# RWKV branch of a hybrid decoder step: the samples' 64 rows move into the prompt's last tile

## The reference, cut to what matters

```
def step(s, inp):
    r_t, w_t, k_t, v_t, kk_t, a_t = inp
    sa = jnp.einsum('bhij,bhj->bhi', s, -kk_t)
    s = s * w_t[:, :, None, :] + sa[..., None] * (kk_t * a_t)[:, :, None, :] + v_t[..., None] * k_t[:, :, None, :]
    return s, jnp.einsum('bhij,bhj->bhi', s, r_t)
...
s_fin, o = lax.scan(step, s_prev.astype(F32), xs)
```

## Time and profile before

| | |
|---|---|
| median of three runs | 2222.6 us |
| the profiled execution | 2221.23 us, span 2219.4 us |
| RWKV block, layer 1, first solve to end | 300.2 to 552 us |
| TensorE, share of the span | 92% |
| VectorE | 48% |
| ScalarE | 31% |
| GpSimd | 10% |
| mean granted TensorE clock | 0.964 of full |

### The profile page before, as it was taken

The page is one execution under the profiler, slowest core; times in us unless marked ns, Lnnn a source line. Parts: engine busy times, 40 slices in busy tenths (PEclk is TensorE's granted clock), DMA queues, the critical chain, the costliest instruction groups (busy, mean ns, idle before and its releaser), DMA issues. The chain is left out here.

```text
span 2219.4 us, 55745 instructions
## 1 busy us (share of the span) xinstructions
PE 2049.8 (92%) x24578; PEld 1330.7 (60%) x24578; DVE 1076.1 (48%) x2577; ACT 682.0 (31%) x1853; POOL 226.4 (10%) x225
## 2 busy tenths in 40 slices
PE   8999978997999999999989999789979999999997
PEld 4665667775566566754456656577754665667543
DVE  2016047674566457833320160477745664588333
ACT  1122044443455442310012220444434554423100
POOL 0000000001000024301100000000010000243022
PEclk9999989997999989999999999899979999899999
DMA  5102010000000337732111020100000003377221
GB/s 199 48 1 85 0 40 4 4 4 22 2 1 1 86 149 277 266 124 71 63 59 48 1 85 1 40 4 4 4 23 1 1 1 86 152 282 258 87 78 57
DMA packets 49843, 150.85 MB, mean 68 GB/s; under 512 B 15106, under 2 KB 19458, under 8 KB 40132
## 3 DMA queue, kind: packets, MB, share of 16 engines
q1 hardware_dynamic: 37316, 71.79, 9.7%
q0 software_dynamic: 12288, 75.51, 9.2%
HBM read 129.70 MB, written 12.86 MB: 64 GB/s over the span
## 5 line engine op out<-in xcount | busy, mean ns | idle before, releaser
L373 PE MATMUL psum<-work 128*128 128x368 f32 (+1 forms) x1632 | 515.3, 477 | 8.9 <-DMA work<-w_z 6.6
L373 PEld LDWEIGHTS psum<-work 128*128 128x128 f32 (+1 forms) x1632 | 308.1, 189 | 212.7 <-issue 26.7
L2191 PE MATMUL psum<-work,mixed 128*128 128x512 f32 (+1 forms) x576 | 252.9, 600 | 1.6 <-PEq L1863 1.6
L2191 PEld LDWEIGHTS psum<-work,mixed 128*128 128x128 f32 (+1 forms) x576 | 107.8, 188 | 140.3 <-issue 140.3
L2059 DVE STREAM_TRANSPOSE work<-work 128x1024 f32<-128x1024 f32 x128 | 150.5, 1214 | 0.4 <-issue 0.3
L1635 ACT ACTIVATE work<-psum,work 128x128 f32<-128x128 f32 (+8 forms) x130 | 97.9, 753 | 160.5 <-DVE work L1738 160.0
L1519 PE MATMUL psum<-work 96*128 96x512 f32 (+3 forms) x384 | 139.6, 498 | 3.7 <-ACT work L1635 2.1
L1803 POOL DMA_INDIRECT work<-cache_ckv,pages x64 | 60.7, 948 | 623.4 <-PE psum L1469 386.4
L1963 PE MATMUL psum<-work,ckv 128*64 128x256 f32 x1024 | 118.0, 382 | 0.7 <-ACT ckv L2018 0.7
L1519 PEld LDWEIGHTS psum<-work 96*128 96x128 f32 x384 | 68.4, 193 | 62.4 <-issue 45.8
L2239 DVE SCALAR_TENSOR_TENSOR work<-work,psum 128x512 f32<-128x512 f32 (+1 forms) x36 | 23.1, 683 | 166.2 <-PE psum L2191 166.2
(11 more groups left out here) (260 smaller groups left out, 3130.5 us busy)
## 6 DMA issues: line engine op xcount, KB each, us to landing
work<-w_z SPq DMA_DIRECT2D x4, 2560.0 KB, 11.3
work<-w_out SPq DMA_DIRECT2D x4, 2048.0 KB, 9.0
xres<-work SPq DMA_DIRECT2D x16, 512.0 KB, 2.9
work<-xT SPq DMA_DIRECT2D x4, 1104.0 KB, 8.9
work<-x_tok SPq DMA_DIRECT2D x8, 512.0 KB, 3.9
work<-xres SPq DMA_DIRECT2D x8, 512.0 KB, 4.2
work<-w_z SPq DMA_DIRECT2D x1, 2304.0 KB, 12.7
o_ckv<-ckv SPq DMA_DIRECT2D x2, 1104.0 KB, 4.3
```

Of the source, the lines that this page charges most:

```text
L373: return nc.tensor.matmul(zb[i % 2][n][rows, 0:G], z_weights(m, g)[:, k, lo:lo + Z_W[i]], xT[:, k, span(n)], start=k == 0, stop=k == DK - 1)
L2191: last = nc.tensor.matmul(yb[t % 2][half][0:n, :], m.mixed[:, k, lo:lo + n], wo[half][:, k, :], start=k == 0, stop=k == DK - 1)
```

## The change

The samples' 64 rows become rows 64 to 127 of tile 8 (chunks 2 and 3, four sequences in each), behind the prompt's 16 rows and 48 rows of padding. RT is 9. Four sequences of 8 rows now share a chunk, and they are kept apart in four ways: by masks of their own for tile 8 (`tail`, loaded by one more DMA into the block's free space); by `flat_m`, zeroed and filled with copies of `wt` and `fm` in which each of four slots holds only one sequence's 8 columns of a chunk, for `read`; by `um` and `vm`, four copies of `u` and `v` in which only one sequence's rows are not zero, for `write`; and by nine columns of decays (`pc_l`) in the place of four. `write` gives the four sequences of a chunk as 256 columns of one product. The shifted row of the inputs (`prev`) comes from a copy of the tile behind `ub`, in which GpSimd sets the samples' first rows.

The diff, cut to its core:

```
-RT = RT_P + NB * CH // P
+RT = RT_P
 RROWS = RT * P
-RS0 = RT_P * P
+RS0 = RROWS - NS
+SEQ_CH = CH // TS
...
+            pool.wait_ge(s_ze, Z_TILES.index("ub1") + 1)
+            nc.gpsimd.tensor_copy(ub[:, :, 1 + RROWS:], ub[:, :, RROWS - P:RROWS]).then_inc(s_shift, 1)
+            pool.wait_ge(s_shift, 1)
...
     def steps(t):
-        if t >= RT_P:
-            return [range(C4)]
-        return [range(c, c + 1) for c in range(C4) if chunk(t, c) < NP_CH]
+        return [range(c, c + 1) for c in range(C4)] if t < LAST_T else [range(1), range(2, C4)]
...
+            sp.dma_start(tail, m.consts[:, C_N:]).then_inc(s_tail, 16)
...
+            def clear(t, _):
+                if t == LAST_T:
+                    pool.wait_ge(s_rkv, 3 * RT)
+                    nc.gpsimd.memset(flat_m, 0.0).then_inc(s_pl, 1)
+                    pool.wait_ge(s_pl, 1)
+
+            def split_values(t, _):
+                if t == LAST_T:
+                    pool.wait_ge(s_tail, 16)
+                    pool.wait_ge(s_rkve, 3 * RT)
+                    pool.wait_ge(s_rd, 2 * steps_to(LAST_T))
+                    nc.gpsimd.tensor_tensor(vm[SMP], of_each(v_sb[SMP, t % 3, :]), own_rows, ALU.mult).then_inc(s_pl, 1)
+                    pool.wait_ge(s_pl, 2)
+            run({"keys_norm": keys_norm, "norm": norm, "sums": clear, "wt": split_values})
...
             def read(t, k):      # TensorE
+                if of_samples(t, k):
+                    pe.wait_ge(s_wte, t + 2)
+                    pe.wait_ge(s_u, steps_to(t) + k)
+                    for i in range(SEQ_CH):
+                        for hf in range(2):
+                            for kind in range(2):
+                                for c in range(2):
+                                    for p in range(2):
+                                        r = slice(64 * p, 64 * p + 64)
+                                        n = kind * P + hf * HD
+                                        last = nc.tensor.matmul(bank[p][rows(2 + c), n:n + HD],
+                                                                masked(kind, hf, i)[r, c * CH:(c + 1) * CH],
+                                                                s_in[r, SEQ_CH * c + i, hf, :],
+                                                                start=i == 0 and hf == 0 and kind == 0, stop=kind == 0,
+                                                                skip_group_check=True)
+                    last.then_inc(s_rd, 2)
+                    return
...
             def write(t, k):     # TensorE
+                if of_samples(t, k):
+                    pe.wait_ge(s_pl, 2)
+                    pe.wait_ge(s_wu, RT)
+                    for c in range(2):
+                        if c == 1:
+                            pe.wait_ge(s_wr, NP_CH + 1)
+                        for hf in range(2):
+                            for p in range(2):
+                                out = bank[4 + hf][64 * p:64 * p + 64, c * 2 * P:(c + 1) * 2 * P]
+                                nc.tensor.matmul(out, bk[rows(2 + c), t % 3, 0, head(hf, p)],
+                                                 um[rows(2 + c), :, head(hf, p)], start=True, stop=False)
+                                last = nc.tensor.matmul(out, bk[rows(2 + c), t % 3, 1, head(hf, p)],
+                                                        vm[rows(2 + c), :, head(hf, p)], start=False, stop=True)
+                        last.then_inc(s_wr, 1)
+                    return
...
             def wts(t, _):       # ScalarE
                 nc.scalar.copy(wt[:, t % 2], bank[6][:, 0:WA]).then_inc(s_wte, 1)
+                if t == LAST_T:
+                    act.wait_ge(s_pl, 1)
+                    for hf in range(2):
+                        for kind in range(2):
+                            src = bank[6][:, hf * P:(hf + 1) * P] if kind == 0 else fm[:, t % 2, hf, P:2 * P]
+                            last = nc.scalar.copy(masked_all(kind, hf),
+                                                  src[:, SMP].rearrange("p (c i x) -> p i c x", c=2, i=SEQ_CH))
+                    last.then_inc(s_wte, 1)
...
             def read(t, k):      # VectorE
+                if of_samples(t, k):
+                    link(last)
+                    last = nc.vector.tensor_tensor(um[SMP], of_each(flat(u)[SMP]), own_rows, ALU.mult)
+                last.then_inc(s_u, 1)
...
             def write(t, k):     # VectorE
+                if of_samples(t, k):
+                    for hf in range(2):
+                        by = pc_l[:, hf, 1:].rearrange("p (c o) -> p c o", o=1).to_broadcast([P, NB, HD])
+                        last = nc.vector.tensor_tensor(s_in[:, :, hf], s_in[:, :, hf], by, ALU.mult)
+                    link(last)
+                    dve.wait_ge(s_wr, NP_CH + 2)
+                    nc.vector.tensor_tensor(s_out[:, 1:], s_in,
+                                            m.psum[:, 4:6, :].rearrange("p f (c j) -> p c f j", j=HD),
+                                            ALU.add).then_inc(s_state, 1)
+                    return
```

More of the change, by code:

```diff
@@ L82 @@
 C_N = C_M8 + TP % P
+L_MI, L_MS, L_GT, L_MX = range(4)
+L_ME = 4 * P
+L_ROW = L_ME + CH
+L_TOT = L_ROW + SEQ_CH
+L_N = L_TOT + 1 + NB
 KEYS = 8
 def constants():
-    c = np.zeros((P, C_N), np.float32)
+    c = np.zeros((P, C_N + L_N), np.float32)
     i = np.arange(P)[:, None]
@@ L109, in constants @@
     row = np.arange(RROWS)
-    held = (row < TP) | ((row >= RS0) & ((row - RS0) % CH < TS))
+    held = (row < TP) | (row >= RS0)
     c[:, C_ROW:C_ROW + RT] = held.reshape(RT, P).T
@@ L115, in constants @@
     c[:, C_M8:C_N] = np.where(j <= i % (TP % P), 0.0, NEG)
+    tail = c[:, C_N:]
+    j = np.arange(P)[None, :]
+    own = np.where(i < P - NS, i // CH, P + i // TS)
+    same = own == np.where(j < P - NS, j // CH, P + j // TS)
+    for n, m in enumerate((i <= j, i < j, i > j)):
+        tail[:, n * P:(n + 1) * P] = m & same
+    in_ch = (i < P - NS) | (s // TS == d // TS)
+    tail[:, L_MX * P:L_ME] = np.concatenate([(s < d) & (s // 16 == d // 16) & in_ch, (s <= d) & in_ch,
+                                             (s < d) & in_ch, (s <= d) & in_ch], axis=1)
+    tail[:, L_ME:L_ROW] = (s // 16 < d // 16) & (i < P - NS)
+    tail[:, L_ROW:L_TOT] = s // TS == np.arange(SEQ_CH)[None, :]
+    tail[:, L_TOT:L_TOT + 1] = i < CH
+    tail[:, L_TOT + 1:] = (i - (P - NS)) // TS == np.arange(NB)[None, :]
     c[:, C_EPS] = 1e-6
@@ L684, in sqc, with sums_of, masks, prev_of @@
         return const[:, n * P:(n + 1) * P]
-    mask_x = sqc(C_MX)
-    mask_e = const[:, C_ME * P:C_ME * P + CH]
+    def sums_of(t):
+        if t == LAST_T:
+            return [tail[:, n * P:(n + 1) * P] for n in (L_MI, L_MS, L_GT)]
+        return [sqc(c) for c in (C_MI, C_MS, C_GT)]
+    def masks(t):
+        if t == LAST_T:
+            return tail[:, L_MX * P:L_ME], tail[:, L_ME:L_ROW]
+        return sqc(C_MX), const[:, C_ME * P:C_ME * P + CH]
+    def prev_of(t, k):
+        return m.ub[:, k, (t + 1) * P + 1:(t + 2) * P + 1] if t == LAST_T else m.ub[:, k, t * P:(t + 1) * P]
+    def masked(kind, hf, i):
+        return flat_m[:, kind, hf, i * 2 * CH:(i + 1) * 2 * CH]
+    def masked_all(kind, hf):
+        return flat_m[:, kind, hf].rearrange("p (i n) -> p i n", i=SEQ_CH)[:, :, 0:2 * CH] \
+            .rearrange("p i (c m) -> p i c m", c=2)[:, :, :, 0:TS]
     ident_c = const[:, C_ME * P + CH:C_ME * P + 2 * CH]
@@ L803, in sums @@
                 pe.wait_ge(s_rkve, 3 * t + 3)
-                for i, c in enumerate((C_MI, C_MS, C_GT)):
-                    nc.tensor.matmul(bank[2 + i // 2][:, (i % 2) * WA:(i % 2 + 1) * WA], sqc(c), logd,
+                if t == LAST_T:
+                    pe.wait_ge(s_tail, 16)
+                for i, c in enumerate(sums_of(t)):
+                    nc.tensor.matmul(bank[2 + i // 2][:, (i % 2) * WA:(i % 2 + 1) * WA], c, logd,
                                      start=True, stop=True)
+                each = tail[:, L_TOT:L_N] if t == LAST_T else sqc(C_B32)[:, 0:P:CH]
+                n = 1 + NB if t == LAST_T else C4
                 for k in range(2):
-                    last = nc.tensor.matmul(bank[3][:, WA + 4 * k:WA + 4 * k + 4], logd[:, k * P:(k + 1) * P],
-                                            sqc(C_B32)[:, 0:P:CH], start=True, stop=True)
+                    last = nc.tensor.matmul(bank[3][:, WA + n * k:WA + n * k + n], logd[:, k * P:(k + 1) * P],
+                                            each, start=True, stop=True)
                 last.then_inc(s_cum, 1)
@@ L1115, in mix @@
                 c = t * P
-                now, prev = m.ub[:, :, 1 + c:1 + c + P], m.ub[:, :, c:c + P]
+                now = m.ub[:, :, 1 + c:1 + c + P]
+                prev = m.ub[:, :, 1 + c + P:1 + c + 2 * P] if t == LAST_T else m.ub[:, :, c:c + P]
                 link(nc.vector.tensor_tensor(du, prev, now, ALU.subtract))
@@ L1253, in write @@
                     last = nc.vector.scalar_tensor_tensor(
```

(2 more changed lines are left out.)

76 lines of the change are left out of this document (38 added, 38 removed).

## The result

The changed kernel takes 2157.9 us in the median of four runs (2151.8 to 2161.7) against 2222.9 of the kernel before: ratio 0.970, 95% interval 0.9668 to 0.9732. The forecast was 2152. So 65 us went where 70.9 were summed; by the interval of the ratio the gain lies between 60 and 74 us, so the times alone don't tell the two apart, and what was off is read from the profiled executions.

A forecast was written before the change was run, and what follows sets the result against it. Full turns were taken as bound by TensorE's list, the rest by the chain through the engines. Per layer 16.0 + 22.6 = 38.6 us replaced 73.76 and 74.30, saving 70.9 in all: 2152 us, range 2141 to 2166.

The forecast's parts named there:

- The rest, 22.6 us: From tile 8's first read to the block's end, a chain through the engines: seven links summed to 22.6 us.
- (b): In the rest, TensorE's read of the samples, 64 matmuls in 128 passes: 2.7 us, bounds 1.5 and 5.4.
- (c): In the rest, VectorE forms u, then um, with TensorE waiting behind it: 1.9 us.
- (d): In the rest, TensorE's write of the samples, twice 16 passes of 256 columns: 4.2 us, bounds 3.4 and 8.5.
- (f): In the rest, finish(7) on VectorE, then up to out with the gate's transposes: 1.7 us.
- (g): In the rest, from out to the block's end, with four gate pieces on VectorE: 8.8 us.
- The clock: Rival: tile 8's read and write run at 1.2 GHz, some 5.5 us more a layer, 2163 us; chance 0.13.
- The solve of tile 8, 16.0 us,: From tile 8's first solve product to its first read: 16.0 us at mixed clock, between 13.7 and 17.5.
- 2 (one row group is one lane): Rival: in the samples' write the column halves don't run together, 8.5 us for 4.2, 2161 us; chance 0.07.
- 3 (GpSimd): Rival: GpSimd's clear or split_values lands on the path, up to 2.5 us a layer, 2157 us; chance 0.07.
- 4 (a tile is worth a tile, 87 us): Rival: the two removed tiles save their full period, 2 x 21.8 us a layer, 2135 us; chance 0.05.
- 5 (passes to one place wait): Rival: the samples' read passes adding to one PSUM place wait for each other, 2239 us, slower; chance 0.02.

The follow-up runs named there:

- experiments 1 and 3: Matrix products nobody reads added to TensorE's list: 1 in the changed kernel, 2139.6 us (0.962); 3 in the kernel before, 2215.9 us (0.9964).
- experiment 6: Changed kernel with the samples' write of chunks 2 and 3 in separate PSUM banks, passes alternating, no wait between: 2149.9 us (0.9683).
- experiment 4: Changed kernel without the samples' state: their read and write left out, states copied unchanged, rows from stale values: 2143.8 us (0.964).
- e3: Changed kernel with GpSimd's two pieces (clearing flat_m, forming vm) done twice: 2155.8 us (0.9708).
- e4: The kernel of experiment 6: changed kernel with the samples' write in two PSUM banks, 2149.9 us (0.9683).
- e5: Changed kernel with unread TensorE products only in the rest after tile 8's solve: 2144.1 us (0.962).
- e7: Changed kernel with the lists after tile 8's solve reordered, out(8) ahead of the samples' write: 2139.5 us (0.9595).
- e10: Changed kernel with the order of e7 and the two banks of e4, without unread products: 2138.7 us (0.9601).
- e1: Changed kernel with unread TensorE products ahead of waits in tile 8's solve and in the rest: 2139.6 us (0.962).
- e9: Changed kernel with unread TensorE products only in tile 8's solve, and one before the first read: 2154.4 us (0.968).
- e8: Changed kernel with the order of e7, the two banks of e4 and unread TensorE products: 2129.7 us (0.9571), the fastest of all.
- experiment 5: The run e3: changed kernel with GpSimd's clearing of flat_m and forming of vm done twice, 2155.8 us (0.9708).

## Why the prediction was right, and where it was off

**The direction and the place** were right: nearly all of it lies in the stretch that was named. Of the span's 62.7 us the two stretches give 61.4. The turns of tile 7 give 3.6 more, and the rest of the program took 2.3 back, 1.6 of it at the start of the prompt block. Where the clock is kept up in both kernels (experiments 1 and 3) the stretches differ by 70.8 us, next to the 70.9 summed. As the kernels stand the profiled stretches are 8.4 and 1.6 us longer than the 38.6 forecast: 5.2 us of it in the two solves, 4.8 in the two rests.

**The rest, 22.6 us.** Layer 2 took 22.71, and most of its links came out as summed: (a) 1.85 for 1.9 (1574.47 to 1576.32), (b) 2.01 for 2.7, (c) 1.8 for 1.9 (the end of the read, 1578.33, to 1580.13), (d) 5.5 for 4.2, (e) 1.22 for 1.4, (f) 1.5 for 1.7 (1586.88 to 1588.35), (g) 8.8 for 8.8 (1588.35 to 1597.18). Two are off: (b) was 0.7 shorter, and (d) 1.3 longer, because the clock fell in its second chunk. That the sum came out to a tenth is partly luck, for the two and some smaller ones cancel. The first chunk of (d), at full clock, took 2.06 for 2.1, but of other parts: its passes run at 0.22 us where 0.265 was taken, and 0.28 us before the next chunk had been left out.

**The clock** was priced as a rival with 0.13, and in layer 1 that is what happened: the rest took 27.3 us, 4.7 more than the sum, where the rival had 5.5. In layer 2 the clock was at half from the second chunk of the write to the end of the block, but only that chunk paid more than was summed, for the end of tile 10, on which (g) was priced, had run at half too. The measured 2157.9 us lies between the forecast and the rival's 2163. The forecast leaned on the one row where tile 10's read and write had met full clock, between 10.2 us of half and 17.0 of half. That row showed one case of where the clock falls and rises. The layers of one run, and the profiles of runs with equal code in the solve (in layer 1 the changed kernel was at half from 483.54 to 527.92, experiment 6's from 481.40 to 501.90 and then near full for 3.4 us), show several. The spread of the runs fits this: in experiment 4 the two fastest runs (2136.2 and 2136.4) have a mean granted clock of 0.963, the slowest (2151.5) 0.953. It is as wide for the kernel before, 2217.8 to 2230.5 over eleven runs.

**The solve of tile 8, 16.0 us,** is the term that was mis-sized: 19.7 and 17.5. It was to hold 10 us of half clock, and no more than 13.7 without any. The mean clock of a window tells how long it was at half: 13.0 us of layer 1's solve, 6.7 of layer 2's. So the clock can explain the excess of layer 1 in part; layer 2 had less of it than was taken and was 1.5 us longer all the same. The kernels e3, e4, e5, e7 and e10 run this solve without unread products, and their profiles show it at other amounts of half clock: 15.8 us with 3.4 at half (e3 and e10, layer 2), 16.8, 17.8, 17.9 and 18.2 with about 10.2 (e7 and e4 in layer 2, e3 in layer 1, e5 in layer 2), 19.4 with 9.4 (e7, layer 1), 19.8 and 20.1 with 15.9 and 15.4 (e10 and e4, layer 1). With the forecast's own 10 us the term was mis-sized by 1 to 2 us, and in layer 1 another 3 us of half clock came on top. With unread products and full clock (e1, e9, e8's layer 1) it took 16.0 to 17.1. Up to one microsecond of it has a row of its own: TensorE stands still in the middle of a group of equal passes, waiting for nothing that the trace shows ("issue"). Layer 2 of the changed kernel:

```profile
1561.23 0.34 PE L918 MATMUL psum<-work 32*32 32x32 f32 x17
1562.58 0.61 PE L918 MATMUL psum<-work 32*32 32x32 f32 x47 [1.02 <-issue]
```

Layer 1 has 0.86 at 481.41. The kernel before has such pauses too, 0.23 to 0.63 us, in some turns and not in others. The turn of tile 10 in layer 1, from which the 16.0 was worked out, has none; the same turn in layer 2 has one of 0.63 (at 1635.35) and takes 16.73 us for 16.43. The traces point at code that comes late: of the pauses of TensorE over 0.4 us in the RWKV blocks of all twelve profiles, 53 in all, every one ends 1.26 to 1.61 us after a 16 KB packet of the queue that the profile calls "instruction" (one such packet ends every 4 to 5 us there). No run varies it, so it is a lead and not shown as the cause.

**The term that was missed** is `mix(9)`, 2.1 us of VectorE ahead of the next solve's first product, in tile 7's turn. I had said that nothing is altered in tiles 0 to 7; but the list of a turn holds work of the tile two ahead. Worth 1.2 us in layer 1.

**The rivals.** 2 (one row group is one lane) is out: 16 passes of 256 columns in one row group take 2.06 us with the wait, 0.11 a pass by the starts, and two lanes of 0.265 / 2 were the forecast's 0.13. 3 (GpSimd) is out by the traces of experiment 5. 4 (a tile is worth a tile, 87 us) is out: the interval ends at 74, and it is 76 at a clock kept up. 5 (passes to one place wait) is out: 128 passes in 2.01 us, 16 ns each, though each place takes eight of them.

**The skill's pages.** The Trainium skill, TensorE: Matmul & The Clock Gate, "What overlaps and what doesn't": by its rule the passes of the write, all in one row group, would each have added their weight load. In 0.48 us four passes of L1042 start, 0.12 each, 0.24 a pass in each of two lanes; later groups start every 0.44 and 0.43, 0.22 a pass. `proj`'s passes of 256 columns, 0.265 us with the gap between groups, are no shorter. Nor are the passes in which another row group stands between, so that a load could hide: L1932's 31 ns over eight places are 0.25 a pass in each, and experiment 6's eight passes every 0.48 us over four places are 0.24. There is no room for the 53 ns that I estimated from that page, and the measurement decides: the load was hidden here.

The prediction also says that no row of this case shows GpSimd and a VectorE instruction with two SBUF inputs starting together. The trace of the kernel before has such a pair; the last section comes back to it.

## What to carry to other kernels

A stretch without dense work can pay in clock for being packed tighter: here the change gave back some 10 of 76 us; look at the granted clock of what will be left, not of what is there, and price the stretch at both levels. In lists made by hand, ask of the last tile what each step truly needs: here the end of the last tile stood behind a state write that it never reads, and moving it was worth 18 us, as much as the unread products. Then look again at each list: VectorE's addition still held up the end of that tile. When work is removed from a software pipeline, walk through the turns ahead of it too, for they hold its first pieces.

## What the hardware showed that I had not expected

Products that nobody reads made the kernel 18 us faster, by the granted clock (in the stretch 0.50 to 0.81 became 0.92 to 1.00, and in the 10 us behind it 0.80 and 0.71 became 1.00), and 9 us faster even in the kernel before, most of it behind the stretch.

Two groups of rows writing two PSUM banks ran at twice the rate of one: eight passes every 0.48 us for four, and at half clock eight every 0.85.

TensorE's pauses in the middle of a group of equal passes follow the packets of the instruction queue: the one before 481.41 ends 1.3 us after such a packet, the one before 1562.58 1.5 us, and the 53 of the twelve profiles 1.26 to 1.61 us.

The power of 4 elements in `norm` takes 1.01 us on GpSimd (all 18 times in the changed kernel), and 1.38 where a VectorE product with both inputs in SBUF runs beside it. From the fastest kernel, GpSimd alone, then VectorE and GpSimd together; last, from the kernel before, the one beside L1245, which starts at 537.43:

```profile
495.25 1.01 POOL L825 TENSOR_TENSOR work<-work,const_sb 128x4 f32<-128x4 f32 x1 [3.89 <-DVE work L1413]
...
501.14 1.29 DVE L1402 TENSOR_TENSOR work<-work 128x512 f32<-128x512 f32 x2
501.32 1.38 POOL L825 TENSOR_TENSOR work<-work,const_sb 128x4 f32<-128x4 f32 x1 [5.05 <-DVE work L1413]
...
537.60 1.38 POOL L763 TENSOR_TENSOR work<-work,const_sb 128x4 f32<-128x4 f32 x1 [15.65 <-DVE work L1266]
```

The Trainium skill, SBUF — State Buffer, "shared port pair", has such pairs exclude each other; the loser waiting for the other's whole instruction. The trace agrees in direction: GpSimd's starts 0.18 us behind the first of VectorE's two and is 0.37 us longer than alone, while the two take 1.29 us, as they do with GpSimd idle (504.75 in the changed kernel). It doesn't show the whole of such a wait: what was left of the first product was 0.5 us. That VectorE's two products have both inputs in SBUF is in their row (work<-work); which of them held GpSimd the row doesn't tell, but in the kernel before there is only one, and the time is the same.
